# Neighbourhood attention: the value products and their evacuation go ahead of the transposes of the step after them

## The reference, cut to what matters

```
s = jnp.einsum('bnqhd,brnchd->bhnqrc', qr, kr).astype(jnp.float32) * scale
s = jnp.where(mask, s + bias.astype(jnp.float32), -jnp.inf)
p = jax.nn.softmax(s.reshape(s.shape[:4] + (-1,)), axis=-1).reshape(s.shape)
o = jnp.einsum('bhnqrc,brnchd->bnqhd', p, vr)
```

## Time and profile before

| | |
|---|---|
| median of 3 runs | 1205.43 us (1205.01 to 1205.53) |
| the profiled execution's own time | 1207.23 us |
| its span, first to last instruction | 1205.6 us |
| PE busy | 1145.1 us, 95% of the span |
| DVE, ACT busy | 644.6 us, 469.7 us |
| the attention's 48 steps | about 366 to 472 us of the span |

### The profile page before, as it was taken

One profiled execution on the slowest core, in us unless ns is written; L12 is line 12 of the kernel. 1 busy time (PEld: TensorE's weight loads), 2 busy tenths in 40 slices (PEclk: granted clock), 3 DMA queues, 4 the chain that ended last, 5 costly groups with the idle time before them and its releaser, 6 DMA issues.

```text
span 1205.6 us, 19051 instructions
## 1 busy us (share of the span) xinstructions
PE 1145.1 (95%) x6884; PEld 918.3 (76%) x6884; DVE 644.6 (53%) x1245; ACT 469.7 (39%) x983; POOL 232.6 (19%) x337
## 2 busy tenths in 40 slices
PE   8999999999998999999999999999986999999956
PEld 6888888878885666888898887778776788887722
DVE  6332333312116896333566663754667998884256
ACT  6333333211015785111333333544224666764223
POOL 2322322200000000000100000100022334554344
PEclk9999999999999999999999999999986999999979
DMA  9573553843148425523222002822896999989967
GB/s 323 131 261 111 146 164 99 291 99 95 48 113 219 110 53 169 184 76 94 63 76 71 1 24 78 300 82 94 330 334 237 370 372 352 358 299 358 405 256 273
DMA packets 108429, 226.61 MB, mean 188 GB/s; under 512 B 28854, under 2 KB 48318, under 8 KB 108222
## 3 DMA queue, kind: packets, MB, share of 16 engines
q1 hardware_dynamic: 83822, 167.86, 41.3%
q0 software_dynamic: 17856, 43.02, 10.7%
q10 hardware_dynamic: 6672, 14.69, 3.9%
HBM read 180.89 MB, written 69.78 MB: 208 GB/s over the span
## 4 chain that ended last, share of the span: by engine, by line
PE 82%; DVE 4%; DMA 4%; issue 3%; SPq 2%; ACT 2%; POOL 1%; DVEq 0%; POOLq 0%; ACTq 0%
PE bank L576 18%; PE bank L578 17%; PE bank L577 17%; PE bank L2361 5%; PE bank L2289 3%; PE bank L2158 3%; PE bank L2327 3%; PE bank L2144 2%; PE bank L2131 2%; PE bank L2347 2%; PE bank L2298 2%; PE bank L2223 2%; PE bank L2399 2%; DMA at<-in_w_in 2%; DVE at L571 1%
## 5 line engine op out<-in xcount | busy, mean ns | idle before, releaser
L576 PE MATMUL bank<-at,at 128*128 128x512 f32 (+1 forms) x1192 | 441.9, 371 | 4.3 <-DVE at L571 2.7
L578 PE MATMUL bank<-at,at 128*128 128x512 f32 (+1 forms) x1192 | 432.0, 362 | 0.0
L577 PE MATMUL bank<-at,at 128*128 128x512 f32 (+1 forms) x1192 | 431.3, 362 | 0.0
L576 PEld LDWEIGHTS bank<-at,at 128*128 128x128 f32 x1192 | 226.1, 190 | 39.0 <-DVE at L571 3.7
L578 PEld LDWEIGHTS bank<-at,at 128*128 128x128 f32 x1192 | 225.9, 189 | 34.9
L577 PEld LDWEIGHTS bank<-at,at 128*128 128x128 f32 x1192 | 226.1, 190 | 32.3
L571 DVE TENSOR_TENSOR at<-at,at 128x1024 fp32r<-128x1024 f32 (+2 forms) x162 | 180.5, 1127 | 104.6 <-ACT at L566 101.8
L566 ACT ACTIVATE at<-at 128x1024 fp32r<-128x1024 f32 (+2 forms) x162 | 154.2, 985 | 165.5 <-DVE at L1545 49.0
L899 POOL TENSOR_TENSOR at<-at 128x1 f32<-128x1 f32 x88 | 24.2, 275 | 553.8 <-ACT at L1264 278.1
L2361 PE MATMUL bank<-at,at 128*128 128x512 f32 x156 | 74.2, 597 | 3.3 <-ACT at L1338 3.3
L995 POOL DMA_INDIRECT y_tok<-at,at x39 | 39.4, 1010 | 132.3 <-DVE at L1902 92.7
(11 more groups left out here) (224 smaller groups left out, 1326.3 us busy)
## 6 DMA issues: line engine op xcount, KB each, us to landing
at<-in_w_exp_gate SPq DMA_DIRECT2D x39, 512.0 KB, 7.6
at<-in_w_exp_up SPq DMA_DIRECT2D x39, 512.0 KB, 11.1
at<-in_w_exp_down SPq DMA_DIRECT2D x39, 512.0 KB, 13.1
at<-y_tok SPq DMA_DIRECT2D x24, 512.0 KB, 10.6
at<-in_w_in SPq DMA_DIRECT2D x6, 1024.0 KB, 11.4
xT_hi_all<-at POOLq DMA_DIRECT2D x12, 512.0 KB, 3.9
xT_lo_all<-at POOLq DMA_DIRECT2D x12, 512.0 KB, 5.7
at<-xT_hi_all SPq DMA_DIRECT2D x3, 2048.0 KB, 10.1
```

What stands on the lines that cost most here:

```text
L576: nc.tensor.matmul(out, w_hi, x_hi, start=(k == 0), stop=False)
L577: nc.tensor.matmul(out, w_lo, x_hi, start=False, stop=False)
L578: last = nc.tensor.matmul(out, w_hi, x_lo, start=False, stop=(k == len(terms) - 1))
```

## The change

PE's list has `values(s-2)` ahead of `transpose_p(s-1)`, and DVE's list has `evac_o(s-2)` ahead of `evac_pT(s-1)`. DVE's subtraction for `w_out_lo` stays behind `evac_pT`, so that it is now the last of DVE's step. ACT's and SP's lists are as they were. No instruction is added or taken away, and no wait is changed.

```diff
@@ DVE @@
                 if s == N_STEPS:
                     evac_yT(0, 0)
+                if s >= 2:
+                    evac_o(s - 2)
                 if 1 <= s <= N_STEPS:
                     evac_pT(s - 1)
                 if s - 1 in W_OUT_STEPS:
                     n, k = W_OUT_STEPS[s - 1]
                     make_lo(dve, split_w_out(n, k), w_out_lo[n][:, k], w_out[n][:, k], w_out_hi[n][:, k])
-                if s >= 2:
-                    evac_o(s - 2)
@@ PE @@
                 if s == N_STEPS:
                     pe.wait_ge(s_biased, 2 * (N_STEPS - 1))
                     transpose_y(0, 0)
+                if s >= 2:
+                    values(s - 2)
                 if 2 <= s <= N_STEPS:
                     transpose_p(s - 1)
-                if s >= 2:
-                    values(s - 2)
```

## The result

The changed kernel is slower. Over 7 runs of each its median is 1210.94 us (1209.18 to 1215.02) against 1205.43 (1203.95 to 1206.27); the ratio is 1.0046, with a 95% interval of 1.0032 to 1.0060. Beside its parts on another chip it was 1.0034 times the kernel before (1.0021 to 1.0047). The forecast, 3.9 us more (a ratio of 1.0032), lies at the lower end of the first interval and inside the second. The profiled execution took 1213.43 us with a span of 1211.8, which is 2.5 us above the median of its kernel.

The account below looks back on a forecast made before the run. It took PE, busy 76.78 of 80 us, and its loop through ACT's copy as the bound; 0 + 0.3 + 2.8 + 0.6 + 0.2 = 3.9 us on the median 1205.43 gives 1209.3 us, range 1205.0 to 1213.0.

Parts of the forecast that it names:

- Same gate for values and transposes: PE, steps 3 to 48: both groups wait for ACT's copy L1184, so swapping them costs 0 per step.
- The passages between PE's groups: PE's changes from group to group in the new order: 0, with ends 2.3 us either way over 46 steps.
- The crossings: Wide transposes and values meeting narrow scores, once per pair of heads: DVE's copy ends later than ACT's, 0.3 us in all.
- The pieces: DVE's 16 pieces of w_out_lo, now directly in front of the next bias, make it late: 2.8 us in all.
- The start: Transposes of step 1 now stand behind the late values(0) at the half clock: scores of step 4 are 0.6 us late.
- The end: Scaling of 46 now precedes DVE's copy, delaying the values of 47 and the next product by 0.2 us.
- the third rival: Start of the attention: the half clock lasts one more stretch, adding 1.7 us, 1211.0 us in all; chance 0.12.
- The first rival: Attention steps: values fill PE's waits, saving some 4 us over the stage, 1201.5 us in all; chance 0.08.

Follow-up runs that it names:

- e7: The changed kernel with DVE's 16 pieces of w_out_lo made behind step 48; steps 10 to 47 took 79.17 us.
- e8: The changed kernel with ACT's copy of the step before between its two exponentials; steps 10 to 47 took 77.07 us, ratio to before 0.9995.
- e10: The kernel before, in its old order, with ACT's copy between the two exponentials; steps 10 to 47 took 78.70 us, ratio 0.9994.
- e6: The kernel before with DVE's 16 pieces of w_out_lo made behind step 48; steps 10 to 47 took 78.95 us.
- e1: The changed kernel with DVE's piece directly behind the bias, ahead of scaling and copy; steps 10 to 47 took 80.33 us, ratio to before 1.0018.
- e0: The changed kernel as it is, run again beside its parts; steps 10 to 47 took 81.88 us, ratio to before 1.0034.
- e4: The changed kernel's order on PE only, DVE keeping its old list; steps 10 to 47 took 84.41 us, ratio to before 1.0049.
- e9: The changed kernel with ACT's copy between the exponentials and step 2 in the old order; steps 10 to 47 took 77.08 us, ratio to before 0.9985.

## Why the prediction was right

*Same gate for values and transposes, 0 per step.* Right. Narrow steps without a piece keep their length to 0.02 us a pair, and e7 has 0.22 us over 37 steps for everything but the pieces. e8 against e10 (77.07 and 78.70) shows the gate from the other side: when the copy comes sooner the new order gains, while with the copy in its old place and without pieces it gains nothing (79.17 in e7, 78.95 in e6).

*The passages between PE's groups, 0.* Nearly: the four steps 12 to 16 take 7.59 us in e7 and in the change, 7.62 before. That is 0.02 less for each narrow pair, and with the next term it leaves about -0.3 over the steps 10 to 47. The Trainium skill (TensorEngine Tiling (Array Packing), Key Properties) says that a change of tiling mode drains TensorE. With three changes per step in either order these traces agree with it, but no run here changes their number, so none tests it.

*The crossings, 0.3.* The mechanism is there, and a little larger. From the scores of 11 to those of 12, of 23 to 24 and of 35 to 36 it takes 2.20 us in e7 and 2.03 in e6: 0.17 three times, 0.5 in all. The fourth lies behind the scores of step 47 and costs nothing there: DVE's evacuation L1545, which comes next on the way, starts 3.17 us behind those scores before and 3.18 in the change. The first of them in the timeline of the change:

```profile
390.95 0.64 PEld L2144 LDWEIGHTS bank<-at,at 128*128 128x128 f32 x6
...
391.75 0.21 PEld L2131 LDWEIGHTS bank<-at 64*64 64x64 f32 x8 [0.17 <-issue]
391.86 0.49 ACT L1184 ACTIVATE at<-bank 128x384 f32<-128x384 f32 x1 [0.29 <-PE bank L2144]
391.86 0.56 DVE L1525 COPY at<-bank 128x384 f32<-128x384 f32 x1 [0.43 <-PE bank L2144]
...
392.49 0.81 PEld L2158 LDWEIGHTS bank<-at,at 128*64 128x64 f32 x24 [0.53 <-ACT at L1184]
```

The values start 392.49 - 390.95 = 1.54 us behind the transposes, where 1.53 was forecast, and 0.07 behind the end of DVE's copy. So e7's 0.22 is about 0.5 for the crossings less 0.3 for the passages, two small misses of opposite sign.

*The pieces, 2.8.* 2.7, by e6, e7 and the change. Step by step, a piece that ACT made in step k shows in the time from the scores of k+3 to those of k+4. The five narrow ones of k = 22, 24, 26, 36 and 38 cost 0.33 each (2.29 in the change, 1.96 in e7), where 0.32 was forecast. The other three narrow ones (33, 34, 39) cost 0.2 together: of two pieces in neighbouring steps the second costs next to nothing, where half a price was forecast. The remaining eight come to 0.8, from 0 to 0.2 each. e1 shows the place on DVE to be the cause, though a piece ahead of the copy has a price of its own: 80.33 against 79.17, 1.2 us.

*The start, 0.6.* With one half-clock stretch of the usual length it is 5.71 us twice in the old order (before, e10), and 6.30 to 6.34 in the new one (e0, e1, e4, e7, e8): 0.6. This compares traces that all have the stretch. If the new order also brings it more often (six traces of six, against four of eight), the order costs more than that on average; so few traces can't show it.

*The end, 0.2.* 5.13 against 4.91. In e4, where the scaling keeps its old place, it is 4.99.

These terms sum to 3.7 us. The profiled execution had 1.0 us more from a longer half clock, which was the third rival (priced at 1.7), 1.1 behind the attention, and 0.4 because the values' transfer landed later (first values at 370.51 in place of 370.13): together the 6.2 us by which its span is longer. The last two are not explained by the change, as far as the runs show. The medians differ by 5.5 in the first comparison and by 4.2 in the second, and both intervals hold 3.9, the first at its very edge; which part of the first median's further 1.6 us is chance stays open. The first rival (the values fill the wait) fell with the listed releaser: the wait is behind L1184.

## What to carry to other kernels

Before an operation is moved into the idle time in front of another, ask what it waits for itself: here both waited for one copy, and the listed releaser was a wait that had ended earlier. A reordering on one engine moves the deadlines on the others: work that lay beside a wait for free (16 pieces on DVE) came to lie in front of the loop's next link and cost 2.7 us. The order pays only if the producers' order goes with it (copy between the exponentials), and then the gain is still small where PE is busy 96% of the time.

## What the runs showed of the hardware

The fall of the clock at the start is not fixed by the length of PE's wait there. With the new order at step 2, PE has one wait of 2.3 to 3.2 us ahead of the first values, and in all six traces the granted clock fell to its half level between 369.4 and 372.1 us, once for 6.8 us and five times for 3.4. In the old order the transposes divide this wait: 0.8 us ahead of them, and 0.3 to 1.2 us ahead of the values. There it fell in four of eight traces, with a last wait of 0.60, 0.62, 0.89 and 1.20 us, and not in the other four, with 0.30, 0.42, 0.86 and 0.91. The Trainium skill (TensorE: Matmul & The Clock Gate, Part 1) puts the half rate down to idleness; the longer wait of the new order goes along with more falls here, but four and four at waits of like length show that such a wait may or may not bring one.

A half-clock stretch of 3.4 us costs 1.0 to 1.3 us in this place (5.71 against 4.44 and 4.46, 7.31 against 6.3). That is less than the 1.7 us that half speed would take by itself, which is an estimate, half of 3.4; that waits hide the rest is likely and not shown. Both traces of e9's program had their stretch at 268 us instead, in the stage before, and reached step 1 later (367.9 and 368.1 us, where the twelve others have 365.9 to 366.6): what they gain at the start they had lost before it.
